# A hybrid attention and expert-retrieval block: U and V of an expert gathered as one row of 8 KB

## The reference

```python
q = (h @ w_q).reshape(Bb, S, PEER_HEADS, 2, PEER_HALF)
scores = jnp.einsum('bshpd,pnd->bshpn', q, sub_keys)
vals, idx = lax.top_k(scores, PEER_TOPK)                 # 16 of 128, twice
cand = vals[..., 0, :, None] + vals[..., 1, None, :]     # 256 pairs, top 16 of them
...
gates = jax.nn.softmax(top_vals, axis=-1)
u = jnp.take(u_tab, e, axis=0)                           # row of 1024 for each expert
act = jax.nn.gelu(jnp.einsum('td,thkd->thk', xt, u))
vv = jnp.take(v_tab, e, axis=0)
y = jnp.einsum('thk,thkd->td', g * act, vv)
```

## Time and profile before

| | |
|---|---|
| median of 3 runs | 3861.61 us (3858.42 to 3883.16) |
| the profiled execution | 3826.47 us, span 3824.7 us |
| mean granted TensorE clock | 0.896 |
| busy: PE, DVE, ACT, POOL | 76%, 68%, 23%, 61% |
| DMA traffic | 1373.44 MB, mean 359 GB/s |

### The profile page before, as it was taken

How to read it: one execution, slowest core, us unless ns; L and a number is a source line. 1 busy time by engine, 2 the same in 40 slices (tenths; PEclk the granted TensorE clock), 3 DMA queues, 4 the chain that set the end, 5 groups by cost and what they waited for, 6 DMA issues and landing times.

```text
span 3824.7 us, 34537 instructions
## 1 busy us (share of the span) xinstructions
PE 2919.9 (76%) x11088; PEld 1913.1 (50%) x11088; DVE 2603.0 (68%) x5403; ACT 893.9 (23%) x1935; POOL 2337.5 (61%) x2052
## 2 busy tenths in 40 slices
PE   8989888568877787788877787867676676667777
PEld 6868657455534464655544454634443443324224
DVE  1144888996677857876768867877668767863541
ACT  2331331221322311222222221121123111121212
POOL 0003565476776766476766767476777777674772
PEclk9989988789978998999989998988898888869998
DMA  6657999899999999899999999899999999997995
GB/s 220 221 203 263 388 356 379 313 403 388 382 412 364 381 371 382 318 382 385 385 375 394 389 387 376 342 369 406 395 408 377 412 412 411 399 367 277 397 373 203
DMA packets 342549, 1373.44 MB, mean 359 GB/s; under 512 B 38737, under 2 KB 40657, under 8 KB 309730
## 3 DMA queue, kind: packets, MB, share of 16 engines
q0 software_dynamic: 294912, 1073.87, 72.9%
q1 hardware_dynamic: 47458, 297.36, 19.8%
HBM read 1362.69 MB, written 8.39 MB: 358 GB/s over the span
## 4 chain that ended last, share of the span: by engine, by line
PE 16%; POOL 15%; issue 9%; DMA 7%; DVE 3%; another core or an unknown queue 2%; ACT 2%; ACTq 0%; DVEq 0%; POOLq 0%
POOL ubuf L431 8%; POOL vbuf L431 7%; PE ysum L673 7%; DMA vbuf<-in_v,idx 5%; PE bank L488 4%; PE bank L497 3%; DMA ubuf<-in_u,idx 1%; DVE ubuf L1133 1%; PE bank L660 1%; ACT diag L885 1%; DVE acc L1159 0%; PE bank L553 0%; DVE tX L1055 0%; PE wide L505 0%
## 5 line engine op out<-in xcount | busy, mean ns | idle before, releaser
L431 POOL DMA_INDIRECT ubuf<-in_u,idx x1024 | 1175.4, 1148 | 1054.0 <-DVE ubuf L1133 535.2
L673 PE MATMUL ysum<-vbuf,diag 128*128 128x512 f32 x2048 | 1157.2, 708 | 685.3 <-DMA vbuf<-in_v,idx 322.4
L1133 DVE SCALAR_TENSOR_TENSOR ubuf<-ubuf,hbuf 128x1024 f32<-128x1024 f32 x1024 | 1246.8, 1222 | 416.4 <-DMA ubuf<-in_u,idx 339.9
L431 POOL DMA_INDIRECT vbuf<-in_v,idx x1024 | 1161.9, 1135 | 381.7 <-issue 294.0
L673 PEld LDWEIGHTS ysum<-vbuf,diag 128*128 128x128 f32 x2048 | 416.2, 219 | 1309.3 <-issue 923.9
L1159 DVE SCALAR_TENSOR_TENSOR acc<-vbuf,dots,acc 128x1024 f32<-128x1024 f32 x505 | 645.5, 1278 | 62.0 <-DMA vbuf<-in_v,idx 38.5
L488 PE MATMUL bank<-hT,slab 128*128 128x256 f32 (+1 forms) x3680 | 674.5, 343 | 12.1 <-DMA slab<-in_slabs 4.9
L488 PEld LDWEIGHTS bank<-hT,slab 128*128 128x128 f32 x3680 | 601.0, 195 | 118.0 <-issue 55.2
L497 PE MATMUL bank<-slab,hT 128*128 128x256 f32 x1408 | 316.2, 384 | 1.1 <-ACT rE L700 0.8
L497 PEld LDWEIGHTS bank<-slab,hT 128*128 128x128 f32 x1408 | 271.4, 193 | 57.7 <-issue 21.6
L885 ACT ACTIVATE diag<-ident,dots 128x128 f32<-128x128 f32 x512 | 189.6, 394 | 370.3 <-PE ysum L673 148.7
(11 more groups left out here) (152 smaller groups left out, 2212.1 us busy)
## 6 DMA issues: line engine op xcount, KB each, us to landing
slab<-in_slabs SPq DMA_DIRECT2D x255, 1024.0 KB
ubuf<-in_u,idx POOLq DMA_INDIRECT x1024
vbuf<-in_v,idx POOLq DMA_INDIRECT x1024
rX<-in_x SPq DMA_DIRECT2D x6, 1024.0 KB, 8.6
hbuf<-x_d SPq DMA_DIRECT2D x8, 512.0 KB
tX<-x_d SPq DMA_DIRECT2D x8, 512.0 KB, 10.4
out<-tX SPq DMA_DIRECT2D x8, 512.0 KB
x_d<-rX SPq DMA_DIRECT2D x3, 1024.0 KB, 4.5
```

What stands on the lines that cost most here:

```text
L431: nc.gpsimd.indirect_dma_start(out=dst, out_offset=None, in_=rows, in_offset=bass.IndirectOffsetOnAxis(ap=idx[:, b, k:k + 1], axis=0)).the ...
L673: ins = mm(ysum[:, c, :], diag[:, m % DS, :], vbuf[:, at % VS, c * 512:c * 512 + 512], start=(m == first), stop=(m == last))
L1133: v.scalar_tensor_tensor(out=row, in0=row, scalar=1.0, in1=hbuf[:, i % 2, :], op0=ALU.mult, op1=ALU.mult, accum_out=dots[:, g % 3, k:k + 1 ...
```

## The change

The two tables are joined on the host, so that U and V of an expert are one row of 8 KB. There is one gather per expert row into ten slots of 8 KB (`NS`), and one `VLAG` less: a V row is used one step (VectorE) or two steps (TensorE) after the dot of its U half. This takes a gelu and a weight operation for the two rows of each step; the softmax shares are divided beforehand (`shares`). ScalarE now runs the stage of step n - 1 where it ran that of step n, behind the diagonals of step n - 2 and the gelu of step n - 1.

```diff
-US, VS, DS = 6, 8, 3
+DS = 3
+NS = 10
+HB = 2
-ON_PE = [(), ODD, ODD, ODD, ODD, ODD, ODD, tuple(range(TOPK))]
-IS_PE = [at % TOPK in ON_PE[at // (NH * TOPK)] for at in range(ROWS)]
+ON_PE = [(), ODD, ODD, ODD, ODD, ODD, ODD, ODD]
+SPARE = 6
+IS_PE = [at % TOPK in ON_PE[at // (NH * TOPK)] and at % (NH * TOPK) >= SPARE for at in range(ROWS)]
-HOSTED = {2: 0, 3: 1, 4: 2}
+GROUPS = ((0, 1), (2, 3), (4, 5), (6,), (7,))
+HOST = {0: 2, 1: 3, 2: 4}
...
+    if s in GUEST:
+        names += ["T0", "wq2", "T1", "wq3", "pg0", "wq4", "pg1", "wq5", "pg2", "wq6", "pg3", "wq7", "pp", "wq8", "T2"]
...
-            for n in range(0, VEND):
...
+            for at in range(ROWS):
+                g, k = divmod(at, TOPK)
+                if k == 0:
+                    pool.wait_ge(idx_ready, g + 1)
+                if at >= NS:
+                    if IS_PE[at - NS]:
+                        pool.wait_ge(v_used_pe, PE_UPTO[at - NS + 1])
+                    else:
+                        pool.wait_ge(v_used_dve, DVE_UPTO[at - NS + 1])
+                nc.gpsimd.indirect_dma_start(
+                    out=uv[:, at % NS, :], out_offset=None, in_=a["uv"],
+                    in_offset=bass.IndirectOffsetOnAxis(ap=idx[:, g % 4, k:k + 1], axis=0)
+                    ).then_inc(uv_in[at % NS], 16)
```

VectorE, the new weights and their place (the dot reads `uv[:, at % NS, 0:D]`, the V row is `uv[:, at % NS, D:2 * D]`):

```diff
+            def weights(n):
+                g, at = divmod(n, STEPS)
+                part = slice(2 * at, 2 * at + 2)
+                dve.wait_ge(gelu_done, n + 1)
+                dve.wait_ge(share_step, 2 * g + 2)
+                v.tensor_tensor(dots[:, g % 3, part], dots[:, g % 3, part], gexp[:, g % 4, part], ALU.mult
+                                ).then_inc(wts_done, 1)
...
                 for at in range(2):
-                    if 0 <= n < UEND:
+                    if 0 <= n < END:
                         dot(2 * n + at)
+                    if at == 0 and 0 <= n - 1 < END:
+                        weights(n - 1)
                     topk_at(n, at)
-                for at in (2 * (n - VLAG), 2 * (n - VLAG) + 1):
-                    if VLAG <= n < VEND and not IS_PE[at]:
+                for at in (2 * (n - 1), 2 * (n - 1) + 1):
+                    if 0 <= at < ROWS and not IS_PE[at]:
                         add_row(at)
...
-                i, within = divmod(n + 8, UEND // NTILE)
-                if within == 0 and 0 <= i < NTILE:
-                    norm_rows(i)
```

ScalarE and TensorE (`gelu(n)` waits for both dots of step n; on TensorE `stage` begins with `add_rows()`, which works off `rows_due`):

```diff
             for n in range(FIRST, LAST + 1):
+                for at in (2 * (n - 2), 2 * (n - 2) + 1):
+                    if 0 <= at < ROWS and IS_PE[at]:
+                        diagonal(at)
+                if 0 <= n - 1 < END:
+                    gelu(n - 1)
                 g, at = divmod(n, STEPS)
-                if at == 0 and 1 <= g <= NHEAD:
-                    gelu(g - 1)
                 if at == 4 and 0 <= g + 2 < NHEAD:
                     peer_exp(g + 2)
-                for s, name in AT_STEP.get(n, []):
+                for s, name in AT_STEP.get(n - 1, []):
                     stage(s, name)
...
-                for at in (2 * (n - VLAG), 2 * (n - VLAG) + 1):
-                    if VLAG <= n < VEND and IS_PE[at]:
-                        add_row(at)
+                rows_due += [at for at in (2 * (n - 2), 2 * (n - 2) + 1) if 0 <= at < ROWS and IS_PE[at]]
                 for s, name in AT_STEP.get(n, []):
                     stage(s, name)
+                add_rows()
```

SyncE, what goes to DRAM and back. `acc` starts as x1 and has two slots, the normed rows h are stored once instead of normed twice, and the tail reads x2 from DRAM. The tail belongs to a group of tiles now (`GROUPS`), no more to a segment:

```diff
-                if at == 2 and n == "rt" and s + 1 < NSEG:
-                    sp.wait_ge(x1_out, 16 * (s + 1))
+                if at == 2 and n == "rt":
                     sp.wait_ge(vec_done, VEC_ORDER[s, "rt"])
+                    sp.dma_start(tiles(h_d, s), h2[:, 0:SEGS[s], :]).then_inc(h_out, 16)
+                if at == 1 and n == f"wq{NH}" and s + 1 < NSEG:
+                    sp.wait_ge(bank_full, USES_END[s, n])
                     sp.dma_start(xs[:, 0:SEGS[s + 1], :], x_rows(s + 1)).then_inc(x_in, 16)
...
+                    for t in tiles_of:
+                        sp.wait_ge(x2_out[t % 2], 16 * (t // 2 + 1))
+                    sp.dma_start(x2[:, 0:tt, :], x2_d[t0:t0 + tt].rearrange("t p d -> p t d")).then_inc(x2_in, 16)
...
+                    sp.dma_start(acc[:, i % 2, :], x1_d[i]).then_inc(acc_in[i % 2], 16)
...
+                    sp.dma_start(hbuf[:, i % HB, :], h_d[i]).then_inc(h_in[i % HB], 16)
+                i, at = divmod(n - 3, PER_TILE)
+                if at == 0 and 1 <= i <= NTILE:
+                    sp.wait_ge(x2_done, i)
+                    sp.dma_start(x2_d[i - 1], acc[:, (i - 1) % 2, :]).then_inc(x2_out[(i - 1) % 2], 16)
```

More of the change, by code:

```diff
@@ new lines, in scaled_pair, with sigmoids @@
+            def scaled_pair(dst, f, tt, gain):
+                for gs in feature_banks(tt):
+                    b = full()
+                    for g in gs:
+                        m = fn(dst[:, f + g, 0:tt * P], b[:, (g - gs[0]) * tt * P:(g - gs[0] + 1) * tt * P], ACT.Copy,
+                               scale=gain[:, f + g:f + g + 1])
+                    m.then_inc(emptied, 1)
+            def sigmoids(slot, f, b0, tt):
+                for gs in feature_banks(tt):
+                    b = full()
+                    for g in gs:
+                        m = fn(gates[:, slot, g, 0:tt * P], b[:, (g - gs[0]) * tt * P:(g - gs[0] + 1) * tt * P],
+                               ACT.Sigmoid, bias=b_bg[:, b0 + f + g:b0 + f + g + 1])
+                    m.then_inc(emptied, 1)
@@ L941, in biased @@
                 first = s == 0 and batch < 2
+                if batch == 0:
+                    dve.wait_ge(emptied, USES_END[s, f"t{SEGS[s] - 1}"])
+                    step(v.memset(probs[:, :, 0:CHUNK], 0.0))
+                else:
+                    dve.wait_ge(emptied, USES_END[s, f"va{batch - 1}"])
                 hd0 = (batch % 2) * 2 * GROUP
@@ L1147, in add_row @@
                 m = DVE_UPTO[at]
-                first = DVE_UPTO[i * NH * TOPK]
-                dve.wait_ge(wts_step, 2 * (g + 1))
+                dve.wait_ge(wts_done, at // 2 + 1)
                 if m:
                     dve.wait_ge(v_used_dve, m)
-                if m == first and i:
-                    dve.wait_ge(x2_done, i)
-                dve.wait_ge(v_in[at % VS], (at // VS + 1) * 16)
-                weight = dots[:, g % 3, k:k + 1]
-                if m == first:
-                    ins = v.tensor_scalar(acc[:], vbuf[:, at % VS, :], weight, None, ALU.mult)
-                else:
-                    ins = v.scalar_tensor_tensor(out=acc[:], in0=vbuf[:, at % VS, :], scalar=weight, in1=acc[:],
-                                                 op0=ALU.mult, op1=ALU.add)
@@ L1161, in add_row @@
-                ins.then_inc(v_used_dve, 1)
+                if m == DVE_UPTO[i * NH * TOPK]:
+                    dve.wait_ge(acc_in[i % 2], 16 * (i // 2 + 1))
+                row = acc[:, i % 2, :]
+                v.scalar_tensor_tensor(out=row, in0=uv[:, at % NS, D:2 * D], scalar=dots[:, g % 3, k:k + 1], in1=row,
+                                       op0=ALU.mult, op1=ALU.add).then_inc(v_used_dve, 1)
             def second_residual(i):
                 last = (i + 1) * NH * TOPK
-                dve.wait_ge(tX_in[i % 2], 16 * (i // 2 + 1))
```

603 lines of the change are left out of this document (303 added, 300 removed).

## The result

The changed kernel takes 3675.14 us (median of 4 runs, 3665.2 to 3678.36) against 3860.02 us; the ratio is 0.951, interval 0.946 to 0.956. The forecast was 3814.

The account below looks back on a forecast made before the run. The prediction took transfer as the bound, except at both ends and in three places. Its terms, -53 + 37 - 25 - 20 + 5 + 8 = -48 us, gave 3778 on the profiled run, 3814 us on the median's scale; range 3725 to 3925.

Parts of the forecast that it names:

- Wider rows: Gathers: 1024 of 1 MB replace 2048 of 512 KB, at the hardware queue's price per MB: -53 us, bounds 0 and -260.
- Added traffic: DRAM transfers: h and x2 written and read back, g_ffn loaded more often, 14.7 MB: +37 us, bounds +25 and +40.
- Slots: Gather buffers: ten slots of 8 KB replace 6 + 8 of 4 KB: 0, bounds -20 and +60.
- VectorE: More V rows (+118 us) and weight operations (at most +105) on this engine, at most 2806 us busy: cost nothing, covered by transfer waits.
- Where stages stand: `wq` steps: the tail of two finished tiles is interleaved with them, removing idle transfer: -25 us, bounds -30 and +10.
- the interleaving: The tail of two finished tiles placed between the `wq` steps, 17 steps in all: -25 us of the 30 idle.
- The stall at 3400 us: Tail of tiles 5 and 6 meeting V rows all on TensorE; tail and rows now split: -20 us of 26, bounds -26 and 0.
- The end: After the last gather: new DRAM round trip, no wait for 25 rows of TensorE, 56 us: +5 us, bounds -5 and +15.
- The start: First change of segment: x is loaded after the last `wq`, so a load of 1 MB comes first: +8 us, bounds 0 and +12.
- Gelu every step: Slower rival: table load and gelu exposed in the first tile and `wq` steps, +147 us, 3961 us; chance 0.18.
- Everything closes: Faster rival: TensorE's waits for V rows go, steady stretch at 400 GB/s, -175 us with +50, 3736 us; chance 0.14.

Follow-up runs that it names:

- two gathers: The changed kernel with each 8 KB slot filled by two gathers of 4 KB rows, U then V: 3779.72 us, ratio 0.987 to the kernel before.

## Why the prediction was wrong

**The bound.** Transfer is the main bound before and after the change: share 0.97 and 0.98, and 281 us of ScalarE's work taken away moved the time by some 10 us. But the share hid a second bound of the kernel before: in the stretches where GpSimd issued without a pause it stayed near 0.98 while the rate fell to a mean of 369 GB/s.

**Wider rows: the term that failed.** The prediction priced the 8 KB packets like the slab queue, 2.547 us per MB, and took -53 us. The gathers came to 2.4515 us per MB, below the slab queue (2.557) itself: -156 us of queue time. On the scale of the profiled runs the forecast was 3778 us and the time 3678; of these 100 us this term alone is 103. Three things were off. First, the price was read over the whole span. In the trace of before the queues of the steady part (400 to 3742 us, packets, MB, share) and the slab queue up to 400 us read

```profile
q0 software_dynamic: 285940, 1041.23, 80.8%
q1 hardware_dynamic: 34910, 222.69, 16.4%
q1 hardware_dynamic: 11972, 71.53, 50.7%
```

The slab queue pays 0.507 x 400 / 71.53 = 2.84 us per MB at the start and 0.164 x 3342 / 222.69 = 2.46 in the steady part, where the gathers pay 2.59. With the steady prices the same working gives (2.593 - 2.461) x 1073.87 = 142 us of gain, near the 156 measured. Second, the sum gave the 1024 gathers fewer nothing, "it hid behind the wait for slots". GpSimd waits for slots in some places and issues without a pause in others; a second set of gathers beside the big packets costs 73 us. The two reasons overlap, since the gathers' 2.59 also holds the stretches where GpSimd sets the pace. Third, the best stretch at 411 GB/s was taken as the limit of the rate: 421 to 422 GB/s is a rate that no slice of before had. The bound of -260 us made from it was not reached.

**Added traffic.** +37 us forecast, 757 to 798 us on the queue: +41. Right.

**Slots.** Forecast at 0 within -20 and +60. Ten slots of 8 KB against 14 of 4 KB was not run by itself; nothing in the steady share (0.97 and 0.98) speaks against 0. Two slots fewer cost 63 us, so the edge is nearer than the text said.

**VectorE.** +118 us of V adds: 645.5 to 763.2, exactly. Weights at most +105: 15.0 to 80.5 us, +65. From 2603 to 2717 us, 74%, and no bound.

**Where stages stand.** -25 us forecast from the interleaving; undone it costs 15, but the stretches where the gain was to be (0.92, 0.86) kept their idle time (0.92, 0.83). The working for 17 dense steps had TensorE, VectorE and transfer within 10% of each other and called that even. With transfer at 2.45 us per MB it isn't: 52 MB are 127 us against 134.

**The stall at 3400 us.** -20 forecast, share 0.74 to 1.01: -26. Of the reason half is not borne out: V rows all on TensorE leave no gap there when the tail is one tile's. VectorE's wait of 36 us in the tail of two tiles points at that tail; it was not run alone.

**The end.** +5 forecast. After the last row landed (VectorE waits for it until 3626.59 us) it is 50 us to the end at 3676.6, where 56 were forecast. From the last gather's issue (3772.51 us before, 3611.37 after) it is 52 and 65 us. The last 77 us with share 0.56 leave 34 us idle, against 41 before. Residual and round trip through DRAM took 7.3 us where 11.8 were forecast, and the backlog of 25 V rows is gone.

**The start.** +8 forecast, the first indices are 16 us later; up to 400 us the share is 0.66 for 0.65, so nothing was lost there.

The idle parts together were forecast at -32 us and measured at -32; that is luck in part, since the interleaving missed its gain and the start and the end cost less than was said.

**The rivals.** Gelu every step: the mechanism is there (158 loads, 146 us of waits), its price is some 10 us in place of 147. The prediction's reason for that, VectorE's other work between dot and weights, was not tested by itself. By total VectorE waits longest for rows (400 us), though its longest single wait is one of 29.4 us for a gelu. A table load took 1.283 us here, as in the trace of before:

```profile
1011.23 0.39 ACT L960 ACTIVATE diag<-ident,dots 128x128 f32<-128x128 f32 x1
1011.64 1.28 ACT L952 ACT_TABLE_LOAD   x1
1012.93 0.20 ACT L952 ACTIVATE dots<-dots 128x2 f32<-128x2 f32 x1
```

The Trainium skill ("ScalarE: Activation LUTs", section Table sets: the hidden batching unit) puts a load at about 2.7 us, which its section What ACT_TABLE_LOAD costs splits into about 1283 ns for the load and about 1380 ns for a drain. This trace agrees with the first; for the second it leaves no room, as the operations before and after stand 0.02 us or less from the load.

Everything closes: 3736 us was the nearest rival, and its steady rate of 400 GB/s came (399). Its means came in part: TensorE's 322 us of waits for V rows are gone, with 502 us of waits for diagonals in their place.

**The scale.** The forecast multiplied nothing but added its 48 us to a median that was 35 us above the profiled run. That part of the miss of 139 us, 35 us, is the difference between runs of the kernel before, not a term.

## What to carry to other kernels

Where transfer is the bound and gathers make most of it, try wider rows first: the price per byte fell by 5.6%, where the slab queue's line over the whole span gave 1.9%. Read a queue's price from the steady part and not from the whole span, and hold the rate in GB/s beside the share, which stays near 1 when the issuing engine is what limits. Count that engine's gaps between gathers as taken. Then look for the places where the plan puts one piece of front in each step: spreading pieces that have no due date was worth some 28 us for one line.

## What the runs showed of the hardware

- A gather of 128 rows took GpSimd a mean of 1.15 us at 4 KB and 1.29 us at 8 KB, 0.94 us at least, and 0.30 us stand between two that wait for nothing.
- With next to no other data on the queues and GpSimd issuing 4 KB rows without a pause, the rate was 350 GB/s at a DMA share of 0.95 (two gathers, 3500 to 3600 us).
- Saturated slices read 410 to 412 GB/s with 4 KB rows, 417 to 420 with 8 KB rows and a small gather behind each, and 421 to 422 with 8 KB rows alone.
- 1024 small gathers of 16 rows x 64 bytes (1 MB in all) lengthened the span by 69 us and the gather queue's busy time by 61. GpSimd's issue and the slightly lower full rate add up to this by an estimate from the trace; neither was tested alone.
- Not all of a faster transfer came out as time: 140 us of queue time were 109 us of the median.
